# Two hybrid mixer blocks on one core: in the forgetting attention VectorE takes a turned tile's low part ahead of the newest maximum, and GpSimd's norm weights of the gating branch stand at other steps

## The chip, the core and the metric

The kernel runs on one core of a Trainium2 chip. TensorE (PE) multiplies matrices into eight banks of PSUM, VectorE (DVE) and ScalarE (ACT) read those banks, GpSimd (POOL) works in SBUF alone, and SyncE (SP) starts the transfers. Each engine takes its own instructions strictly in the order in which the program lists them; between engines there are only semaphores. The metric is the device time in microseconds (us) of one execution, lower is better.

## The reference, cut to what matters

The whole computes two blocks of width 1024 over 512 tokens, in fp32: a gated delta rule with windowed attention, and then a block with forgetting attention, a chunked spatial gating branch and a convolved feed-forward. The change touches the second block's attention and its gating branch:

```python
def forgetting_attention(q, k, v, log_f):          # 8 heads of 64, 4 query blocks of 128
    c = jnp.cumsum(log_f, axis=1)
    def block(args):
        logits = jnp.einsum('bqhd,bkhd->bhqk', qi, k).astype(jnp.float32) * scale
        logits = logits + ci[..., None] - c_k
        logits = jnp.where(causal, logits, -jnp.inf)
        p = jax.nn.softmax(logits, axis=-1).astype(v.dtype)
        return jnp.einsum('bhqk,bkhd->bqhd', p, v)

def chunked_spatial_gating(u, vg, v_gain, w_s, b_s):
    vg = rmsnorm(vg, v_gain.reshape(G, Dg))        # v_gain: the "norm weights"
    w = w_s * jnp.tril(jnp.ones((CHUNK, CHUNK), dtype=w_s.dtype))
    mixed = jnp.einsum('gij,bnjgd->bnigd', w, vc) + b_s.T[None, None, :, :, None]
    return (u * mixed.reshape(B, S, G, Dg)).reshape(B, S, G * Dg)
```

## The kernel before, in words

Every large product is made exact enough by splitting both factors into a high part (rounded) and a low part (the rest): three matmuls in place of one. ScalarE copies a weight unit's high part (`wh`), GpSimd subtracts it from the raw unit for the low part (`wl`, line 1149), four slots in a ring.

The order of all work is one Python list, ORDER, written out by hand: `do("name", ...)` appends a step, and each engine later runs those steps of the list that it has a function for. So the place of a `do` in the list sets the place of its instructions on every engine at once. A name that only one engine knows moves that engine alone.

The forgetting attention works through 32 tiles n (head n // 4, query block 3 - n % 4, so that the key widths go 512, 384, 256, 128 and again). The loop has 36 steps (lines 942 to 959). For tile n there are these pieces, which the text below calls by letters:

- S(n), TensorE: scores into bank 4 or 5, four matmuls, the last `bank<-nub,idb` (the causal mask). It waits for the exponential of tile n - 2, which reads the same bank.
- M(n), VectorE line 2073: the negated maximum of each row (`mx`).
- E(n), ScalarE: the exponential `p<-bank,mx` with its row sum `dn`. It waits for M(n).
- R(n), VectorE line 2079: the reciprocal of the sum. N(n), GpSimd line 1251: `p<-p,dn`, the normalised tile.
- T(n), TensorE line 2176: p is turned (transposed, `bank<-consts,p`) into bank 6, at step n + 3. It waits for N(n) and, since there is one bank for it, for L(n - 1).
- H(n), ScalarE: the high part of the turned tile (`pth<-bank`). L(n), VectorE: its low part (`ptl<-bank,pth`), which waits for H(n). Both stand at step n + 3, as T(n) does.
- O(h), TensorE: the product with v for head h (`bank<-pth,vv` and `ptl,vv`), at step 4h + 7. It waits for L(4h + 3). ScalarE and VectorE then add its two halves (`att`).

After these, each step holds "sides": one or two quarters of a dense projection (6 matmuls of 512 columns each), and what comes with it: a weight unit's `wh` and `wl`, or the high and low parts of new queries and keys (`qs`, `kh`, `kl`). The gating branch's own steps come from a generator, `gmlp`: squares, sums, then `gm_gain` four times (GpSimd line 1273, `vg<-vg,rparams`), then the root and the norm. On ScalarE a step therefore reads H(n - 3), E(n), and then `wh` or the copies of the sides; on VectorE M(n), L(n - 3), R(n - 1) and then the sides.

Of the kernel before, what the change touches and what calls it, by code (L numbers as in the profile page):

```python
# [197 lines left out]
def program(nc, x, xt, wflat, cfd, ppd, prd, wsd, tbd, seld, out):  # L198
# [176 lines left out]
    def mark(name):  # L375
        marks.append(Mark(nc, name))
        return marks[-1]
# [15 lines left out]
    resid = mark("resid")  # L393
# [36 lines left out]
    do = lambda *a: ORDER.append(a)  # L430
# [19 lines left out]
    def step(g, n=1):  # L450
        for _ in range(n):
            if next(g, "end") == "end":
                return False
        return True

    def in_turn(*gs):
        for g in gs:
            yield from g
# [440 lines left out]
    def qk_units(j):  # L899
        for what in range(2):  # L900
            u = U_QK2[j] + what
            w_ahead(u + 2)
            G.take(("ch", u), (qk_lo, ("k" if what else "q", j)))
            for part in range(4):
                do("ch_part", u, "n1", part)
                if part == 3:
                    do("qk2", j, what)
                    if what:
                        do("twice", j)
                yield  # L910
# [12 lines left out]
    for n, _ in enumerate(in_turn(qk_units(0), qk_units(1))):  # L923
        if n == 3:
            G.take("cum_a", (fg_a, "lt"))
            do("cum_a")
        if n == 7:
            G.take("cum_b", (fg_v, "c"))
            do("cum_b")
        if n == 11:  # L930
            G.over((0, 1, 2, 3))
        if n == 13:
            for b in FA_S + (FA_T, FA_O):
                BANK[("fa", b)] = (b, emptied[b])
            assert BANK[("ch", U_QK2[1] + 1)][0] not in FA_S + (FA_T, FA_O)
            do("fa_s", 0)
    pace = {n: 2 for n in range(7)}
    pace.update({7: 4, 8: 1, 9: 2, 10: 1, 11: 1, 12: 1})
    pace.update({13: 1, 14: 1, 15: 2})
# [2 lines left out]
    for n in range(36):  # L942
        if 0 < n < 32:
            do("fa_s", n)
        if n > 6 and n % 4 == 3:
            do("fa_o", n // 4 - 1)
        if 3 <= n < 35:
            do("fa_t", n - 3)
        if n < 32:
            do("fa_exp", n)  # L950
        if 1 <= n < 33:
            do("fa_norm", n - 1)
        if 8 <= n < 28 and n % 2 == 0 or n > 32:
            step(gg)
        step(sides, pace.get(n, 0))
        if n in (28, 30, 32):
            do("fa_split", n // 2 - 14)
        if n in (29, 31, 33):
            do("fa_low", n // 2 - 14)
# [80 lines left out]
    def pt_at(tile, qb):  # L1040
        return tile[:, 0:qb + 1, qb * 128:(qb + 1) * 128] if qb < 3 else tile[:, 1:5, 0:128]

    def pt_from(n):
        qb = 3 - n % 4
        return psum[turn_bank(n)][:, 0:(qb + 1) * 128].rearrange("p (k n) -> p k n", n=128)
# [609 lines left out]
    def vector_engine(e):  # L1655
        on = On(e)

        def tt(out_, a, b, op, up):
            return e.tensor_tensor(out_, a, b, op).then_inc(up, 1)  # L1659
# [407 lines left out]
                on.wait_ge(*qk_hi.at(("k", j, 1)))  # L2067
                tt(l[64:128, 1, :], bot, k[64:128, 1, :].bitcast(F32), ALU.subtract, qk_lo.up(("k", j)))

        def fa_s(n):  # L2070
            qb, h = 3 - n % 4, n // 4
            on.wait_ge(*fa_p.at(("s", n)))
            e.tensor_reduce(MX2[:, qb, h:h + 1], psum[FA_S[n % 2]][:, 0:(qb + 1) * 128], AX.X, ALU.max, negate=True).then_inc(
                fa_v.up(("mx", n)), 1)
# [3 lines left out]
            on.wait_ge(*fa_a.at(("p", n)))  # L2078
            e.reciprocal(d, d).then_inc(fa_v.up(("r", n)), 1)  # L2079

        def fa_t(n):
            qb = 3 - n % 4
            on.wait_ge(*fa_a.at(("pt", n)))
            if n % 4 == 0 and n:
                on.wait_ge(*fa_p.at(("o", n // 4 - 1)))
            tt(pt_at(PTL, qb), pt_from(n), pt_at(PTH, qb).bitcast(F32), ALU.subtract, fa_v.up(("pt", n)))
# [51 lines left out]
        def finish(tb):  # L2138
# [12 lines left out]
            for n in range(tb // 3, 2):  # L2151
# [3 lines left out]
        return dict(begin=begin, x_split=x_split, conv_rms=conv_rms, scale=scale, split=split, masks=masks, conv=conv, qexp=qexp, gate_dt=gate_dt, gate_beta=gate_beta, gate2=gate2, rope_tables=rope_tables, rope_sq=rope_sq,  # L2155
                    rope_root=rope_root, rope=rope, rope_keys=rope_keys, rope_k=rope_k, rope_t=rope_t, inv_decay=inv_decay, inv_mb=inv_mb, inv_q=inv_q, inv_m=inv_m,
                    inv_mt=inv_mt, inv_x=inv_x, inv_d=inv_d, inv_x7=inv_x7, inv_t=inv_t, swa_s=swa_s, swa_o=swa_o,
                    scan_ks=scan_ks, scan_s=scan_s, scan_oq=scan_oq, scan_out=scan_out, dn_mul=dn_mul, tok=tok, resid=resid_, fa_const=fa_const, forget=forget, cum_b=cum_b, qk2=qk2, fa_s=fa_s,
                    fa_norm=fa_norm, fa_t=fa_t, fa_o=fa_o_, fa_last=fa_last, gm_sum=gm_sum, gm_rec=gm_rec, gm_norm=gm_norm, gm=gm, up_post=up_post, a_prep=a_prep,
                    finish=finish)  # L2160

    def tensor_engine(e):
# [427 lines left out]
        def down_last(tb):  # L2592
# [4 lines left out]
            for n in range(2):  # L2597
                for k in range(18 if tb else 21, 22):
# [6 lines left out]
                    scan_s=scan_s, scan_av=scan_av, cum_a=cum_a, cum_b=cum_b, fa_s=fa_s, fa_t=fa_t, fa_o=fa_o_, gm=gm, down=down, down_last=down_last)  # L2605

    engines = (tensor_engine, scalar_engine, vector_engine, pool_engine, sync_engine)

    def run(engine, e):
# [10 lines left out]
    with nc.Block() as block:  # L2620
        @block.sync
        def _(e):
            run(sync_engine, e)

        @block.scalar
        def _(e):
            run(scalar_engine, e)

        @block.vector
        def _(e):  # L2630
            run(vector_engine, e)

        @block.gpsimd
        def _(e):
            run(pool_engine, e)

        @block.tensor
        def _(e):
            run(tensor_engine, e)
# [37 lines left out]
```

## Time and profile before

| what | us |
|---|---|
| median of 3 runs (923.84 to 924.92) | 923.9 |
| the profiled execution itself | 923.39 |
| its span, first to last instruction | 921.6 |
| TensorE busy | 906.2 (98% of the span) |
| VectorE busy | 481.8 (52%) |
| ScalarE busy | 457.4 (50%) |
| GpSimd busy | 464.1 (50%) |

The profiled execution lasts 1.8 us longer than its span, and lies 0.5 us under the median of the three runs. The attention loop with its tail lies between 393 and 502 us of the span. A matmul that waits shows the idle time before it in brackets; the start times of two matmuls in a row show the whole delay, since the idle time counts only from the modelled end of the one before.

### The profile page before, as it was taken

The numbers are of one execution on the slowest core, as the hardware profiler recorded it, in microseconds if no ns is written. First come the engines' busy times: TensorE is split into PE (matmuls) and PEld (weight loads), VectorE is DVE, ScalarE is ACT, GpSimd is POOL, SyncE is SP. The second block draws the span as 40 slices with busy tenths as digits, with TensorE's granted clock in tenths as the row PEclk, the third lists the DMA queues.
The fourth block names the chain that finished last, engine by engine and source line by source line (L and its number), as shares of the span: only waits on it lengthen the run. The fifth ranks groups of instructions, "written<-read, shape, count | busy, mean of one in ns | idle before, by whom it ended". The sixth has DMA issues, their size and how long they took to land.

```text
span 921.6 us, 11979 instructions
## 1 busy us (share of the span) xinstructions
PE 906.2 (98%) x4752; PEld 763.7 (83%) x4752; DVE 481.8 (52%) x814; ACT 457.4 (50%) x817; POOL 464.1 (50%) x262
## 2 busy tenths in 40 slices
PE   9999999999999999999999999999999999999997
PEld 6988868899999888788777889888888888888885
DVE  4679836898857443533654434333333334654434
ACT  6666587576546444447557245333343433433223
POOL 4453432987566433456786426444444444344440
PEclk9999999999999999999999999999999999999999
DMA  9522310000022714332221214233222233232202
GB/s 344 191 91 91 97 42 1 1 1 2 2 92 68 267 46 137 115 92 70 75 86 46 97 60 132 101 104 101 92 92 92 91 96 110 73 133 93 91 23 92
DMA packets 25303, 83.63 MB, mean 91 GB/s; under 512 B 3008, under 2 KB 3264, under 8 KB 25120
## 3 DMA queue, kind: packets, MB, share of 16 engines
q1 hardware_dynamic: 24240, 81.49, 26.4%
q10 hardware_dynamic: 1008, 1.38, 0.4%
q8 instruction: 38, 0.62, 0.3%
q14 instruction: 17, 0.14, 0.0%
HBM read 78.66 MB, written 2.10 MB: 88 GB/s over the span
## 4 chain that ended last, share of the span: by engine, by line
PE 81%; DVE 9%; POOL 5%; ACT 3%; DMA 1%; issue 1%; SPq 0%; DVEq 0%; ACTq 0%
PE bank L2168 78%; PE bank L2176 3%; DVE qk L1665 2%; DVE vc L1665 1%; POOL mb L1161 1%; POOL wl L1149 1%; DVE r L1659 1%; ACT L1290 1%; DMA xt<-in_xt 1%; POOL mb L1165 1%; POOL p L1251 1%; POOL dd L1171 1%; DVE bank L1659 0%; ACT vc L1290 0%; ACT xh L1290 0%
## 5 line engine op out<-in xcount | busy, mean ns | idle before, releaser
L1149 POOL TENSOR_TENSOR wl<-raw,wh 128x1024 fp32r<-128x1024 f32 (+1 forms) x129 | 310.3, 2410 | 364.0 <-ACT wh L1290 364.0
L2168 PE MATMUL bank<-xh,wh 128*128 128x512 f32 (+1 forms) x536 | 206.8, 386 | 0.0
L2168 PE MATMUL bank<-xl,wh 128*128 128x512 f32 (+1 forms) x536 | 205.2, 383 | 0.0
L2168 PE MATMUL bank<-xh,wl 128*128 128x512 f32 (+1 forms) x528 | 202.2, 383 | 0.0
L1290 ACT ACTIVATE wh<-raw 128x1024 fp32r<-128x1024 f32 (+2 forms) x132 | 136.0, 1035 | 123.9 <-PE bank L2168 117.8
L2168 PE MATMUL bank<-wh,xh 128*128 128x512 f32 (+1 forms) x352 | 140.5, 399 | 0.8 <-POOL wl L1149 0.4
L2168 PE MATMUL bank<-wh,xl 128*128 128x512 f32 (+1 forms) x352 | 134.5, 382 | 0.0
L2168 PE MATMUL bank<-wl,xh 128*128 128x512 f32 (+1 forms) x352 | 134.1, 381 | 0.0
L2168 PEld LDWEIGHTS bank<-xh,wh 128*128 128x128 f32 x536 | 100.8, 188 | 19.3 <-issue 0.2
L2168 PEld LDWEIGHTS bank<-xl,wh 128*128 128x128 f32 x536 | 100.8, 188 | 19.2
L2168 PEld LDWEIGHTS bank<-xh,wl 128*128 128x128 f32 x528 | 99.2, 188 | 19.6
L2168 PEld LDWEIGHTS bank<-wh,xh 128*128 128x128 f32 x352 | 66.3, 188 | 15.5 <-POOL wl L1154 1.7
L1659 DVE TENSOR_TENSOR al<-ac,ah 128x512 fp32r<-128x512 f32 x22 | 53.6, 2450 | 45.8 <-ACT ah L1290 45.8
L2168 PEld LDWEIGHTS bank<-wh,xl 128*128 128x128 f32 x352 | 66.1, 188 | 13.0
L2168 PEld LDWEIGHTS bank<-wl,xh 128*128 128x128 f32 x352 | 66.4, 189 | 11.8 <-issue 1.0
L1665 DVE SCALAR_TENSOR_TENSOR ta<-bank,pparams,ta 128x510 f32<-128x510 f32 (+1 forms) x44 | 32.9, 749 | 74.1 <-ACT ta L1290 73.3
L2168 PE MATMUL bank<-wh,ah 128*128 128x512 f32 x176 | 68.5, 389 | 0.0
L2168 PE MATMUL bank<-wl,ah 128*128 128x512 f32 x176 | 68.5, 389 | 0.0
L2168 PE MATMUL bank<-wh,al 128*128 128x512 f32 x176 | 68.5, 389 | 0.0
L1665 DVE SCALAR_TENSOR_TENSOR tgg<-bank,pparams,tgg 128x510 f32<-128x510 f32 (+1 forms) x44 | 33.0, 749 | 62.4 <-ACT tgg L1290 61.6
L1290 ACT ACTIVATE tgg<-bank,pparams 128x512 f32<-128x512 f32 x22 | 17.2, 781 | 78.8 <-PE bank L2168 78.8
L1251 POOL TENSOR_SCALAR p<-p,dn 128x512 f32<-128x512 f32 (+3 forms) x32 | 34.8, 1089 | 16.8 <-DVE dn L2079 16.7
(271 smaller groups left out, 1424.7 us busy)
## 6 DMA issues: line engine op xcount, KB each, us to landing
raw<-in_wflat SPq DMA_DIRECT2D x126, 512.0 KB, 3.5
xt<-in_xt SPq DMA_DIRECT2D x8, 256.0 KB, 4.4
h<-in_x SPq DMA_DIRECT2D x4, 512.0 KB, 8.1
h<-in_x SPq DMA_DIRECT2D x1, 2048.0 KB, 8.3
gain<-in_pr SPq DMA_DIRECT2D x3, 512.0 KB, 5.0
consts<-in_cf SPq DMA_DIRECT2D x1, 1088.0 KB, 10.5
raw<-in_wflat SPq DMA_DIRECT2D x4, 272.0 KB, 11.0
kh<-kh SPq DMA_DIRECT2D x8, 128.0 KB, 2.3
```

What stands on the lines that cost most here:

```text
L1149: e.tensor_tensor(WL[u % NS][:, 0:n], RAW[u % NS][:, 0:n], WH[u % NS][:, 0:n].bitcast(F32), ALU.subtract).then_inc(w_lo.up(u), 1)
L1161: e.tensor_tensor(h3(mb), h3(mb), bc4((cf("SL"), cf("SU"))[d]), ALU.mult).then_inc(inv_g.up(("mb1", cb, d)), 1)
L1165: e.tensor_tensor(both, both, mb, ALU.add).then_inc(inv_g.up(("mb", cb)), 1)
L1171: e.tensor_tensor(h3(W["DD"][:, lower(d)]), h3(raw(cb)), bc4(cf("LM", d)), ALU.mult).then_inc(inv_g.up(("dd", cb, 0, d)), 1)
L1251: e.tensor_scalar(p, p, DN2[:, qb, h:h + 1], None, ALU.mult).then_inc(fa_g.up(n), 1)
L1290: return e.activation(out_, in_, f, **k).then_inc(up, 1)
L1659: return e.tensor_tensor(out_, a, b, op).then_inc(up, 1)
L1665: return e.scalar_tensor_tensor(out_, a, s, b, op0, op1).then_inc(up, 1)
L2168: return e.matmul(o, l, r_, start=start, stop=stop, skip_group_check=part)
L2176: return e.transpose(o, in_, cf("ident")[0:in_.shape[0], 0:in_.shape[0]])
```

## The change

On VectorE the step `fa_s` is now called `fa_mx` (the maximum) and `fa_t` is called `fa_tl` (the low part), so that they can be placed apart from TensorE's and ScalarE's steps of the old names. In the steps n with n % 4 other than 3 the low part L(n - 3) now stands ahead of M(n); where n % 4 is 3 it stays behind M(n). TensorE's, ScalarE's and SyncE's orders are as before. On GpSimd the four `gm_gain` move from steps 20, 22, 24 and 26 to 21, 23, 25 and 27.

```diff
             do("fa_s", 0)
+            do("fa_mx", 0)
...
     for n in range(36):
         if 0 < n < 32:
             do("fa_s", n)
+        if 3 <= n < 35 and n % 4 != 3:
+            do("fa_tl", n - 3)
+        if 0 < n < 32:
+            do("fa_mx", n)
         if n > 6 and n % 4 == 3:
             do("fa_o", n // 4 - 1)
         if 3 <= n < 35:
             do("fa_t", n - 3)
+        if 3 <= n < 35 and n % 4 == 3:
+            do("fa_tl", n - 3)
         if n < 32:
             do("fa_exp", n)
         if 1 <= n < 33:
             do("fa_norm", n - 1)
-        if 8 <= n < 28 and n % 2 == 0 or n > 32:
+        if 8 <= n < 20 and n % 2 == 0 or 20 < n < 29 and n % 4 == 1 or n in (23, 27) or n > 32:
             step(gg)
...
-        def fa_s(n):
+        def fa_mx(n):
...
-        def fa_t(n):
+        def fa_tl(n):
```

VectorE, steps 12 to 14 of the loop, before: `mx2` is a maximum M, `ptl` a low part L (from bank 6), `dn2` a reciprocal R, `kl0` the low part of new keys.

```order
L1659 TENSOR_TENSOR ptl_242<-bank6,pth_241 128x4x128
L2079 RECIPROCAL dn2_140<-dn2_140 128x1
L2073 TENSOR_REDUCE mx2_139<-bank4 128x1
L1659 TENSOR_TENSOR ptl_242<-bank6,pth_241 128x3x128
L2079 RECIPROCAL dn2_140<-dn2_140 128x1
L2100 TENSOR_REDUCE vss_138<-vsq0_239 128x8
L1659 TENSOR_TENSOR kl0_230<-bank2,kh0_228 64x512 x2
L2073 TENSOR_REDUCE mx2_139<-bank5 128x1
L1659 TENSOR_TENSOR ptl_242<-bank6,pth_241 128x2x128
```

And the same place now, from the same first row:

```order
L1666 TENSOR_TENSOR ptl_242<-bank6,pth_241 128x4x128
L2086 RECIPROCAL dn2_140<-dn2_140 128x1
L1666 TENSOR_TENSOR ptl_242<-bank6,pth_241 128x3x128
L2080 TENSOR_REDUCE mx2_139<-bank4 128x1
L2086 RECIPROCAL dn2_140<-dn2_140 128x1
L2107 TENSOR_REDUCE vss_138<-vsq0_239 128x8
L1666 TENSOR_TENSOR kl0_230<-bank2,kh0_228 64x512 x2
L1666 TENSOR_TENSOR ptl_242<-bank6,pth_241 128x2x128
L2080 TENSOR_REDUCE mx2_139<-bank5 128x1
```

L(9) (3 x 128 wide) has moved ahead of M(12), and L(10) (2 x 128) ahead of M(13); the reciprocal behind each pair keeps its place.

GpSimd, steps 19 to 24, before: `p20` to `p23` are the norms N, `wl3` a weight unit's low part, `vg` a norm weight.

```order
L1251 TENSOR_SCALAR p23_246<-p23_246,dn2_140 128x128
L1273 TENSOR_TENSOR vg_234<-vg_234,rparams_63 128x512
L1149 TENSOR_TENSOR wl3_60<-raw3_52,wh3_56 128x1024
L1251 TENSOR_SCALAR p20_243<-p20_243,dn2_140 128x512
L1251 TENSOR_SCALAR p21_244<-p21_244,dn2_140 128x384
```

And now:

```order
L1251 TENSOR_SCALAR p23_246<-p23_246,dn2_140 128x128
L1149 TENSOR_TENSOR wl3_60<-raw3_52,wh3_56 128x1024
L1251 TENSOR_SCALAR p20_243<-p20_243,dn2_140 128x512
L1273 TENSOR_TENSOR vg_234<-vg_234,rparams_63 128x512
L1251 TENSOR_SCALAR p21_244<-p21_244,dn2_140 128x384
```

The norm weight has gone behind the weight unit's low part and N(20).

## Rows read from the trace of the kernel before

**Rows 1.** The page, part 1: busy us, share of the span, instructions.

```profile
PE 906.2 (98%) x4752; PEld 763.7 (83%) x4752; DVE 481.8 (52%) x814; ACT 457.4 (50%) x817; POOL 464.1 (50%) x262
```

**Rows 2.** TensorE's waits, 390 to 510 us: total us, times, longest.

```profile
PE bank L2176 <- DVE ptl L1659: 1.5, 4, 0.5
```

**Rows 3.** Timeline, steps 15 to 17: start us, us, engine, line, operation, [idle before].

```profile
452.63 1.41 DVE L1665 SCALAR_TENSOR_TENSOR qs<-bank,qs 64x512 fp32r<-64x512 f32 x2 [1.80 <-ACT qs L1290]
...
454.07 0.69 DVE L2073 TENSOR_REDUCE mx<-bank 128x1 f32<-128x512 f32 x1
...
454.80 0.56 DVE L1659 TENSOR_TENSOR ptl<-bank,pth 128x384 fp32r<-128x384 f32 x1
454.80 0.69 ACT L1290 ACTIVATE p<-bank,mx 128x512 f32<-128x512 f32 x1 [1.07 <-DVE mx L2073]
454.81 0.22 PE L2168 MATMUL bank<-nub,idb 128*128 128x128 bf16 x1
...
455.41 0.44 PE L2176 MATMUL bank<-consts,p 128*128 128x128 f32 x2 [0.38 <-DVE ptl L1659]
455.48 1.05 ACT L1290 ACTIVATE wh<-raw 128x1024 fp32r<-128x1024 f32 x1
...
456.83 0.42 DVE L1659 TENSOR_TENSOR ptl<-bank,pth 128x256 fp32r<-128x256 f32 x1 [0.36 <-ACT pth L1290]
...
457.50 0.28 PE L2176 MATMUL bank<-consts,p 128*128 128x128 f32 x1
```

**Rows 4.** Timeline, steps 28 to 30.

```profile
484.89 0.49 PE L2176 MATMUL bank<-consts,p 128*128 128x128 f32 x3
...
485.95 0.56 DVE L1659 TENSOR_TENSOR ptl<-bank,pth 128x384 fp32r<-128x384 f32 x1 [0.16 <-ACT pth L1290]
...
487.44 0.62 ACT L1290 ACTIVATE xh<-att 128x512 fp32r<-128x512 f32 x1
...
488.37 0.42 DVE L1659 TENSOR_TENSOR ptl<-bank,pth 128x256 fp32r<-128x256 f32 x1 [0.42 <-ACT pth L1290]
...
489.17 0.22 PE L2168 MATMUL bank<-nub,idb 128*128 128x128 bf16 x1
489.23 0.28 PE L2176 MATMUL bank<-consts,p 128*128 128x128 f32 x1
```

**Rows 5.** Timeline, steps 12 to 15.

```profile
440.41 0.52 PE L2176 MATMUL bank<-consts,p 128*128 128x128 f32 x3 [0.15 <-POOL p L1251]
...
442.35 1.21 ACT L1290 ACTIVATE kh<-bank 64x512 fp32r<-64x512 f32 x2 [0.22 <-PE bank L2168]
...
442.97 1.41 DVE L1659 TENSOR_TENSOR kl<-bank,kh 64x512 fp32r<-64x512 f32 x2 [0.27 <-ACT kh L1290]
...
445.00 0.42 DVE L1659 TENSOR_TENSOR ptl<-bank,pth 128x256 fp32r<-128x256 f32 x1
445.00 0.58 ACT L1290 ACTIVATE p<-bank,mx 128x384 f32<-128x384 f32 x1 [1.04 <-DVE mx L2073]
...
445.48 0.33 PE L2176 MATMUL bank<-consts,p 128*128 128x128 f32 x1 [0.54 <-DVE ptl L1659]
...
446.82 0.29 DVE L1659 TENSOR_TENSOR ptl<-bank,pth 128x128 fp32r<-128x128 f32 x1 [1.01 <-ACT pth L1290]
...
447.31 0.48 PE L2168 MATMUL bank<-pth,vv 128*128 128x512 f32 x1
```

**Rows 6.** Timeline of ScalarE, steps 6 and 8.

```profile
418.22 0.48 ACT L1290 ACTIVATE p<-bank,mx 128x256 f32<-128x256 f32 x1
...
429.74 1.28 ACT L1290 ACT_TABLE_LOAD   x1
```

**Rows 7.** Timeline of GpSimd: steps 8 and 20.

```profile
428.64 2.39 POOL L1149 TENSOR_TENSOR wl<-raw,wh 128x1024 fp32r<-128x1024 f32 x1 [3.38 <-ACT wh L1290]
...
466.76 1.31 POOL L1273 TENSOR_TENSOR vg<-vg,rparams 128x512 f32<-128x512 f32 x1
```

**Rows 8.** Timeline of TensorE, step 23.

```profile
472.03 0.66 PE L2176 MATMUL bank<-consts,p 128*128 128x128 f32 x4 [0.61 <-POOL p L1251]
```

More of the change, by code:

```diff
@@ L2157, in vector_engine @@
                     inv_mt=inv_mt, inv_x=inv_x, inv_d=inv_d, inv_x7=inv_x7, inv_t=inv_t, swa_s=swa_s, swa_o=swa_o,
-                    scan_ks=scan_ks, scan_s=scan_s, scan_oq=scan_oq, scan_out=scan_out, dn_mul=dn_mul, tok=tok, resid=resid_, fa_const=fa_const, forget=forget, cum_b=cum_b, qk2=qk2, fa_s=fa_s,
-                    fa_norm=fa_norm, fa_t=fa_t, fa_o=fa_o_, fa_last=fa_last, gm_sum=gm_sum, gm_rec=gm_rec, gm_norm=gm_norm, gm=gm, up_post=up_post, a_prep=a_prep,
+                    scan_ks=scan_ks, scan_s=scan_s, scan_oq=scan_oq, scan_out=scan_out, dn_mul=dn_mul, tok=tok, resid=resid_, fa_const=fa_const, forget=forget, cum_b=cum_b, qk2=qk2, fa_mx=fa_mx,
+                    fa_norm=fa_norm, fa_tl=fa_tl, fa_o=fa_o_, fa_last=fa_last, gm_sum=gm_sum, gm_rec=gm_rec, gm_norm=gm_norm, gm=gm, up_post=up_post, a_prep=a_prep,
                     finish=finish)
```

## The prediction

> **What bounds the kernel now.** I read the page first: TensorE is busy for 98% of the span [rows 1], so almost nothing can be won but the moments in which a matmul waits, and whatever makes TensorE wait longer is lost in full. Then TensorE's waits in the stretch of the attention loop, the only one where the change moves anything: four turns T wait for VectorE's low part L, 1.5 us in all [rows 2], and two for GpSimd's norm N, 0.15 and 0.61 us [rows 5, 8]. Last the timelines of all engines around these waits, where the reader is to see two things.
>
> First, why L comes late. In step 16 VectorE takes the new queries' low part, then M(16), then L(13), and T(14) stands still for L(13) [rows 3]. The idle time shown is 0.38 us, but the last matmul ahead of T(14) starts at 454.81 and T(14) at 455.41; with nothing to wait for, T follows that matmul by 0.06 us (489.17 and 489.23 in step 30 [rows 4]). So the real price is 0.54 us. Step 20 repeats the pattern to a hundredth. In step 13 it is T(11) at 445.48 behind L(10) at 445.00, with keys in place of queries, and costs 0.7 us (0.54 idle and the same hidden 0.16) [rows 5].
>
> Second, what M feeds. E(16) starts in the instant in which M(16) ends, having waited 1.07 us for it; `wh` follows E, the copy H(14) follows `wh`, L(14) follows H at 456.83, and it ends at 457.25, only 0.25 us ahead of T(15) [rows 3]. So M(16) begins a chain over ScalarE that leads back to the next turn, and the slack of this chain is 0.2 us.
>
> **The change, part by part.** Nothing is added or removed; 24 low parts and 24 maxima change places in pairs, and four norm weights move by a step each. Per pair L gains the time of M (0.69 us at 512 columns) and M loses the time from its own readiness to L's end. Where H(n - 3) is not ready, which is the usual case, M no longer runs in that shadow: it waits for T, H and L. All sums are start to start.
>
> 1. The waits that go. With L(13) at 454.07, where M(16) was, it ends at 454.63, ahead of T(14)'s free place at 454.87: -0.54 in step 16, -0.53 in step 20 [rows 3].
>
> 2. The same steps, one turn later. M(16) now starts behind L(13), 0.5 us later (0.56 less a small overlap, an estimate), at 454.57. From M to E 0.73, E to `wh` 0.68, `wh` to L(14) 1.35, L(14) to its turn 0.48 [rows 3, 5]: T(15) can start at 457.81. Its free place is 0.54 ahead of the 457.50 of before, at 456.96. So it waits 0.85, and the two steps together are 0.31 us worse than before. Steps 20 and 21 likewise: +0.85.
>
> 3. Steps 24 and 28, where before nothing waited. The loop is now T to L 1.06 [rows 4], L to M 0.5, M to E 0.73, E to `wh` 0.68, `wh` to L 1.35, L to T 0.48: 4.80 us for two turns. TensorE needs 489.23 - 484.89 = 4.34 [rows 4]. Step 24: +0.46. In step 28 a copy `xh` stands between `wh` and H: `wh` to `xh` is 0.95 (its 1.05 less the overlap), `xh` to L(26) 0.93 [rows 4], in place of 1.35, so the loop is 5.33: +0.99.
>
> 4. Step 12 to 15. The loop there runs through keys: T(9) to L(9) 1.06, then M(12) 0.5, E 0.73, the copies `kh` 0.68, `kl` 0.62 behind (442.35 to 442.97), L(10) 1.44 behind that, T(11) 0.48 [rows 3 to 5]. That is 5.51 from T(9). From 440.41 it gives 445.92 where T(11) was at 445.48 [rows 5]: +0.44, although the wait for M is gone. Then E(13), at 445.00 before, is late by 1.9 (0.5 late from the move, the rest from L(10)), and with it `wh`, H(11) and L(11), which stood at 446.82: it ends at 449.0. O(2) needs it, and its free place is 447.31 + 0.97 = 448.28 [rows 5]. So O(2) waits +0.8. (The 0.97 is this 0.44 and the 0.53 of point 5.)
>
> 5. Upstream of that. E(6) at 418.22 followed H(3) at once and now waits for L(3) and M(6) too, 0.2 (0.29 less an overlap) and 0.42 by the lengths of an L of these widths [rows 3, 5], about 0.6, less 0.1 for which ScalarE idles afterwards. From there to the `wh` for which GpSimd waits at 428.64 ScalarE has almost no gap, and from 428.64 to N(9) GpSimd has none; T(9) already waits for N(9) by 0.15 [rows 5 to 7]. So T(9) comes +0.53 later. From both sides: 0, if ScalarE has slack that I don't see, and 0.6.
>
> 6. Norm weights. T(20) waits 0.61 for N(20) [rows 8], since GpSimd puts a norm weight of 1.31 ahead of the weight's low part and N(20) [rows 7]. Behind N(20) it is out of the way. Most of the wait goes, -0.6: not more, as point 2 makes `wh` and so GpSimd's own loads late in the same step. The other three have slack on both sides of a step: 0. If ScalarE's lateness took all of the freed time, this would be 0.
>
> Sum: -0.54 - 0.53 + 0.85 + 0.85 + 0.46 + 0.99 + 0.44 + 0.8 + 0.53 - 0.6 = +3.25 us. The profiled execution took 923.39, so 926.6 by its own measure; the median of the runs is 0.5 above it, which makes 927.1, and I state 927.0. Behind the loop TensorE runs on without waits of this size, so nothing gives the time back.
>
> One cover deserves a word. In step 8 ScalarE loads its exponential table, 1.28 us from 429.74 [rows 6], while M(8) runs behind L(5); both are ready within 0.1 us of each other, so I cost step 8 at nothing. The Trainium skill (ScalarE: Activation LUTs, "What ACT_TABLE_LOAD costs") gives a switch 2.66 us, the load and a drain. The row shows the load alone; by the page M(8) would be covered with over a microsecond to spare, and the sum would be the same but its rival below, a load that waits for M, dearer: 2.66 in place of 1.28.
>
> **The rivals.** *The waits simply go (faster).* L is what T waits for, so L first is right, and ScalarE absorbs the later E. Then TensorE wins 0.54 + 0.53 + 0.59 (step 13: from `kl`'s end at 444.38 VectorE ran M(13) until L(10) at 445.00 [rows 5]) + 0.6 for N(20), 2.3 us: 921.6 by the median. For it: three of the four waits are of this kind [rows 2], and VectorE and ScalarE are half idle over the span [rows 1]. Against it: it needs E(16) late by 0.5 to leave L(14) in time, and L(14) has 0.25 [rows 3]. It decides from there: a lateness of E under 0.2 us costs nothing, above it all goes to the next turn.
>
> *Losses and gains cancel (no change).* Points 4 and 5 lie upstream of each other; if the `kh` copies of step 12 get ahead, or ScalarE has slack, what is left is -1.07 + 1.70 + 1.45 - 0.6 - 0.59 = +0.9 us: 924.8. For it: 1.8 us of my sum hang on two delays that feed each other. Against it: ScalarE takes its work in order, and in step 12 E(12) stands ahead of `kh` in a place where `kh` had waited only 0.22 for TensorE [rows 5].
>
> *The lateness compounds (slower still).* N is late as well in steps 19, 23 and 28, since `wh` carries GpSimd's `wl` with it: 0.2 each, and the table load in step 8 waits for M(8), 1.28 more [rows 6]. That gives 3.25 + 0.6 + 1.28 = 5.1: 929.0. Against it: nothing in the order ties the load to M.
>
> **How the numbers follow.** Forecast 0.62, faster 0.12, cancelling 0.17, compounding 0.09. A measurement of this kernel tells about 0.2%, 1.8 us, from no change. The forecast's own range is 925.5 to 928.4: 1.5 off if T(9) does not slip (0.5), O(2) slips by half (0.4) and the two loops of point 3 are 0.3 shorter each, 1.4 on if the norms slip too (0.6) and ScalarE frees nothing in point 6 (0.6) and hands on another 0.2. To leave out no more than 2 in 10 the range reaches down through part of the cancelling case and up into the compounding one: 923.5 to 928.8. Slower by over 0.2% (above 925.7) takes the compounding case and nearly all of the forecast, 0.70; within 0.2% takes the cancelling case and a little of the forecast, 0.17; faster 0.13.
>
> **What would show it.** In the profile after: M(16), M(20), M(24), M(28) start behind L and not ahead of it; E waits for M in every step but the fourth; T(14) and T(18) show no wait, but T(15), T(19), T(23) and T(27) wait for L by 0.4 to 1.0 us; O(2) waits for L(11); TensorE's waits for L grow from 1.5 us in 4 to some 4 us in 8 or so, and those for N shrink only if point 6 outweighs point 5. The forecast is wrong if T(15) starts without a wait, or if T(9) stays where it was and T(11) comes earlier.

## The result, and the profile after

The changed kernel takes 927.08 us (median of 7 runs, 926.48 to 928.77) against 924.04 us (7 runs) for the kernel before, run beside it. The ratio is 1.0031, with a 95% interval of 1.002 to 1.0042: 1.8 to 3.9 us slower. The prediction said 927.0 and slower with a chance of 0.70. The profiled execution took 926.48 us, 3.1 more than that of before.

From the page of the changed kernel, the line that answers to [rows 1]:

```profile
PE 906.0 (98%) x4752; PEld 763.6 (83%) x4752; DVE 480.0 (52%) x814; ACT 457.8 (50%) x817; POOL 464.4 (50%) x262
```

TensorE does the same work; it stands still for longer. Its waits between 390 and 514 us (total us, times, longest), against the 1.5 us for L of [rows 2]:

```profile
PE bank L2183 <- DVE ptl L1666: 3.6, 6, 1.0
PE bank L2175 <- DVE ptl L1666: 0.8, 2, 0.6
PE bank L2183 <- POOL p L1258: 0.3, 1, 0.3
```

Four waits for a low part have become eight (L2183 is a turn T, L2175 a product O), and the two for a norm [rows 5, 8] have become one, that of T(9). T(20) no longer waits.

All kernels of this study do the same work in the same order up to T(0), and yet T(0) stands at 406.53 us before, at 406.33 after, and as late as 410.13 in another kernel's trace. So I measure each turn from T(0) of its own trace. In the loop two traces of different kernels then agree to 0.01 us up to T(7), and to 0.06 us up to T(26) where nothing ahead of it was changed. The table gives how much later than before (a minus: earlier) some turns and products start, counted so; 0 stands for 0.03 and less. Its first column is the running sum that the prediction's terms give, the others are the changed kernel and the kernels of the experiments below.

| | predicted | after | low parts alone | weights alone | three steps | wh one later | low, wh two later | wh two later | best |
|---|---|---|---|---|---|---|---|---|---|
| O(1) | 0 | +0.39 | +0.39 | 0 | 0 | +0.38 | +0.38 | 0 | 0 |
| T(9) | +0.53 | +0.52 | +0.54 | 0 | 0 | +0.52 | +0.52 | 0 | 0 |
| T(11) | +0.97 | +0.93 | +0.95 | 0 | -0.62 | +0.92 | +0.93 | 0 | -0.61 |
| O(2) | +1.77 | +1.71 | +1.73 | 0 | +0.16 | +0.93 | +0.92 | 0 | -0.61 |
| T(14) | +1.23 | +1.19 | +1.25 | 0 | -0.34 | +0.40 | +0.41 | 0 | -1.14 |
| T(15) | +2.08 | +2.01 | +2.06 | 0 | +0.47 | +0.35 | +0.35 | 0 | -1.20 |
| O(3) | +2.08 | +2.06 | +2.11 | 0 | +0.52 | +1.10 | +0.35 | 0 | -1.20 |
| T(18) | +1.55 | +1.63 | +1.70 | 0 | +0.12 | +0.55 | -0.23 | -0.06 | -1.78 |
| T(19) | +2.40 | +2.45 | +2.51 | 0 | +0.93 | +0.50 | -0.28 | -0.07 | -1.84 |
| T(20) | +1.80 | +1.86 | +2.06 | -0.74 | +0.49 | +0.50 | -1.05 | -0.83 | -2.61 |
| T(23) | +2.26 | +2.28 | +2.48 | -0.72 | +0.49 | +1.05 | -1.08 | -0.88 | -2.63 |
| T(27) | +3.25 | +3.23 | +3.58 | -0.92 | +0.49 | +1.76 | -1.28 | -1.08 | -2.83 |
| O(7) | +3.25 | +3.28 | +3.65 | -0.91 | +0.50 | +4.29 | -0.20 | -1.07 | -2.82 |

After O(7) nothing moves: from there to the end of the span it is 422.1 us in both traces (921.6 - 499.50 and 924.7 - 502.58). In the other traces the span from T(0) to the end, too, is longer or shorter by what the last row says, within 0.11 us.

The prediction, and one expectation below, speak of 24 maxima and low parts that change places. It is 21 pairs: in steps 32 to 34 there is a low part and no maximum. No term of the sum uses the number.

The timeline of steps 15 to 17 after, to be laid beside [rows 3]:

```profile
454.16 1.41 DVE L1672 SCALAR_TENSOR_TENSOR qs<-bank,qs 64x512 fp32r<-64x512 f32 x2 [1.80 <-ACT qs L1297]
...
455.61 0.56 DVE L1666 TENSOR_TENSOR ptl<-bank,pth 128x384 fp32r<-128x384 f32 x1
...
456.08 0.68 DVE L2080 TENSOR_REDUCE mx<-bank 128x1 f32<-128x512 f32 x1
...
456.40 0.39 PE L2183 MATMUL bank<-consts,p 128*128 128x128 f32 x2
...
456.80 0.69 ACT L1297 ACTIVATE p<-bank,mx 128x512 f32<-128x512 f32 x1 [1.53 <-DVE mx L2080]
...
457.47 1.05 ACT L1297 ACTIVATE wh<-raw 128x1024 fp32r<-128x1024 f32 x1
...
458.42 0.37 ACT L1297 ACTIVATE pth<-bank 128x256 fp32r<-128x256 f32 x1
...
458.83 0.42 DVE L1666 TENSOR_TENSOR ptl<-bank,pth 128x256 fp32r<-128x256 f32 x1 [1.41 <-ACT pth L1297]
...
459.31 0.33 PE L2183 MATMUL bank<-consts,p 128*128 128x128 f32 x1 [0.71 <-DVE ptl L1666]
```

The row to see is T(14), 456.40: it has lost its wait in brackets, as the change wants. Follow the others down: L(13), M(16) at its heels, E(16) which idled 1.53 us for it (1.07 before), `wh`, H(14), L(14), and T(15) now waits 0.71 for that. From the first `qs` row to T(15) it is 5.15 us; before it was 4.87, wait of T(14) included.

### The profile page after: what moved, and what is told of

It reads as the page before. It is cut to its first block, busy times and chain, and to the rows that moved or that the text cites. A ratio compares the mean times of both kernels' runs of the same rounds, so it can differ in the third digit from the quotient of the medians.

```text
span 924.7 us, 11979 instructions
## 1 busy us (share of the span) xinstructions
PE 906.0 (98%) x4752; PEld 763.6 (83%) x4752; DVE 480.0 (52%) x814; ACT 457.8 (50%) x817; POOL 464.4 (50%) x262
## 4 chain that ended last, share of the span: by engine, by line
PE 79%; DVE 10%; ACT 5%; POOL 4%; issue 1%; DMA 1%; SPq 0%; DVEq 0%; ACTq 0%
PE bank L2175 76%; PE bank L2183 3%; DVE qk L1672 2%; DVE vc L1672 1%; POOL mb L1168 1%; ACT L1297 1%; ACT wh L1297 1%; DVE r L1666 1%; POOL wl L1156 1%; DVE ptl L1666 1%; POOL mb L1172 1%; DMA xt<-in_xt 1%; POOL dd L1178 1%; ACT p L1297 1%; DVE bank L1666 0%
## 5 line engine op out<-in xcount | busy, mean ns | idle before, releaser
L2175 PE MATMUL bank<-xh,wh 128*128 128x512 f32 (+1 forms) x536 | 206.8, 386 | 0.0
L2175 PE MATMUL bank<-xl,wh 128*128 128x512 f32 (+1 forms) x536 | 205.2, 383 | 0.0
L2175 PE MATMUL bank<-xh,wl 128*128 128x512 f32 (+1 forms) x528 | 202.2, 383 | 0.0
L2175 PE MATMUL bank<-wh,xh 128*128 128x512 f32 (+1 forms) x352 | 140.3, 399 | 1.6 <-DVE xl L1672 1.3
L2175 PE MATMUL bank<-wh,xl 128*128 128x512 f32 (+1 forms) x352 | 134.5, 382 | 0.0
L2175 PE MATMUL bank<-wl,xh 128*128 128x512 f32 (+1 forms) x352 | 134.1, 381 | 0.0
L2175 PEld LDWEIGHTS bank<-xh,wh 128*128 128x128 f32 x536 | 100.9, 188 | 19.5 <-issue 0.2
L2175 PEld LDWEIGHTS bank<-xl,wh 128*128 128x128 f32 x536 | 100.8, 188 | 19.2
L2175 PEld LDWEIGHTS bank<-xh,wl 128*128 128x128 f32 x528 | 99.3, 188 | 19.4
L2175 PEld LDWEIGHTS bank<-wh,xh 128*128 128x128 f32 x352 | 66.4, 189 | 15.7 <-POOL wl L1161 2.1
L2175 PEld LDWEIGHTS bank<-wh,xl 128*128 128x128 f32 x352 | 66.1, 188 | 13.1
L2175 PEld LDWEIGHTS bank<-wl,xh 128*128 128x128 f32 x352 | 66.3, 188 | 11.6 <-issue 1.0
L2175 PE MATMUL bank<-wh,ah 128*128 128x512 f32 x176 | 68.5, 389 | 0.0
L2175 PE MATMUL bank<-wl,ah 128*128 128x512 f32 x176 | 68.5, 389 | 0.0
L2175 PE MATMUL bank<-wh,al 128*128 128x512 f32 x176 | 68.5, 389 | 0.0
```

The costliest lines, as they stand in the source:

```text
L2175: return e.matmul(o, l, r_, start=start, stop=stop, skip_group_check=part)
```

## The experiments

Each diff is against the changed kernel, and each table value is counted from T(0), as above.

### Low parts alone

```diff
-        if 8 <= n < 20 and n % 2 == 0 or 20 < n < 29 and n % 4 == 1 or n in (23, 27) or n > 32:
+        if 8 <= n < 28 and n % 2 == 0 or n > 32:
```

> Low parts ahead of the maxima as in the changed kernel, the four norm weights left where they were. Chain theory (a late maximum delays the exponential, the weight's high part, the next high part H, the next low part L, the next turn T): slower than before by 3.3 + 0.4 = 3.7 us; T(20) comes 2.2 us later than before (1.9 in the changed kernel), as the norm weight again stands ahead of the weight's low part and N(20), but ScalarE's lateness had already used up most of that room. Rival (GpSimd and the moved norm weights make the loss): no slower than before, since the waits for L at T(11), T(14), T(18) go: -1.7 us.

Measured: ratio 1.0047 (1.0035 to 1.0059), +4.3 us; by the table +3.65, of which T(20) +2.06. The loss is that of the low parts. Counted from the turn before, the norm weights' move saves 0.14 us at T(20) and 0.15 at T(24) (the two columns are 0.06 apart already at T(19), from T(13) on, where no norm weight has moved), not the 0.6 that I had put down for it. The row of the changed kernel in step 20, and then three of this one:

```profile
469.71 2.37 POOL L1156 TENSOR_TENSOR wl<-raw,wh 128x1024 fp32r<-128x1024 f32 x1 [1.07 <-ACT wh L1297]
```

```profile
469.89 0.61 POOL L1258 TENSOR_SCALAR p<-p,dn 128x128 f32<-128x128 f32 x1 [2.27 <-DVE dn L2086]
470.46 1.28 POOL L1280 TENSOR_TENSOR vg<-vg,rparams 128x512 f32<-128x512 f32 x1
471.71 2.37 POOL L1156 TENSOR_TENSOR wl<-raw,wh 128x1024 fp32r<-128x1024 f32 x1
```

In the changed kernel GpSimd idles 1.07 us for the late `wh`. Here it runs the norm weight (1.25 us, start to start) in that time. So nearly all of the wait at T(20) was gone by T(19)'s own lateness.

### Norm weights alone

```diff
-        if 3 <= n < 35 and n % 4 != 3:
+        if 3 <= n < 35 and False:
...
-        if 3 <= n < 35 and n % 4 == 3:
+        if 3 <= n < 35 and not (False):
```

> Norm weights moved alone, maxima ahead of low parts as before. Chain theory: the wait of 0.61 us (0.72 start to start) at T(20) goes and 0.2 at T(24): 0.7 to 0.9 us faster than before, at the edge of what can be measured. Rival (the norm weights carry the loss): slower by 1 to 3 us.

Measured: ratio 0.9996 (0.9987 to 1.0004), -0.4 us and not to be told from nothing; in the trace T(20) is 0.74 and T(24) 0.89 us earlier, and all behind them. As expected, and no rival to the low parts. T(20) without its wait, against [rows 8]:

```profile
471.22 0.66 PE L2183 MATMUL bank<-consts,p 128*128 128x128 f32 x4
```

### The swap only where a turn had waited

```diff
-        if 3 <= n < 35 and n % 4 != 3:
+        if 3 <= n < 35 and n in (13, 16, 20):
```

with the other condition its negation, and norm weights as before.

> The low part goes ahead of the maximum only in steps 13, 16 and 20, the three where TensorE waited for a low part behind a maximum; norm weights as before. Chain theory: each wait goes and comes back larger one turn or product later: O(2) +0.2, T(15) +0.3, T(19) +0.3, so 0.8 us slower than before, with T(11), T(14), T(18) without a wait and O(2), T(15), T(19) with one. Rival (the swap is good where a turn waited and bad only where it was made for nothing, as in steps 6, 9, 12, 24 and 28): 0.59 + 0.54 + 0.53 = 1.7 us faster than before.

Measured: ratio 1.001 (1.0001 to 1.0019), +0.9 us; by the table +0.50. The rival falls: three waits taken away, and the kernel is no faster. Two of the waits that came in their place (O(2) and T(15)):

```profile
447.65 0.50 PE L2175 MATMUL bank<-pth,vv 128*128 128x512 f32 x1 [0.58 <-DVE ptl L1666]
...
458.15 0.33 PE L2183 MATMUL bank<-consts,p 128*128 128x128 f32 x1 [0.71 <-DVE ptl L1666]
```

T(11) is 0.62 earlier and O(2) 0.16 later; T(14) gains 0.54 on T(13) (+0.20), and T(15) loses 0.81. I had said +0.8. At T(19) it is +0.93, of which 0.18 lie between T(15) and T(16) (+0.65), which starts as N(16) ends; this I had left out. T(20) gives 0.44 back, as it would have waited for N(20) anyhow.

### The weight's high part one quarter later, then two

The chain theory says that the 0.95 us of `wh` between E and H are what closes the loop. So the changed kernel was run with the weight units' steps (load, `wh`, `wl`) from step 13 on listed one quarter of a projection later:

```diff
-            w_ahead(u + 2)
+            if u < 51:
+                w_ahead(u + 2)
             G.take(("ch", u), (qk_lo, ("k" if what else "q", j)))
             for part in range(4):
+                if part == 1 and u >= 51:
+                    w_ahead(u + 2)
...
-            w_ahead(u0 + i + 2)
+            if u0 != U_U2:
+                w_ahead(u0 + i + 2)
             for tb in range(4):
+                if tb == 1 and u0 == U_U2:
+                    w_ahead(u0 + i + 2)
```

> The changed kernel with one edit: from step 13 on the weight unit's load, high and low part (ScalarE, GpSimd) are listed one quarter of a projection later, so that ScalarE makes H and the next exponential ahead of the weight's high part. Chain theory: the 0.95 us of the high part leave the chain from maximum to next turn; the loop of steps 24 and 28 is 3.9 us against TensorE's 4.3, so T(15), T(19), T(23), T(27) and O(2) stop waiting, and N(20), N(24) stand ahead of the weight's low part. Left is +0.97 up to T(11) less 0.54, 0.53, 0.72 and 0.18: 1.0 us faster than before, 4 us faster than the changed kernel. Rival (the swap itself costs, through late maxima and norms, whatever ScalarE does next): still 2 to 3 us slower than before.

Measured: ratio 1.0052 (1.004 to 1.0064), +4.8 us; by the table +4.29. This expectation failed. The turns that I had named do stop waiting (T(15) +0.35 in place of +2.01, and T(19), T(23), T(27) by the table). But `wh` now stands one place further down ScalarE's queue, between E(17) and H(15), and the head's product needs L(15):

```profile
458.73 0.58 ACT L1303 ACTIVATE p<-bank,mx 128x384 f32<-128x384 f32 x1 [0.96 <-DVE mx L2086]
...
459.30 1.04 ACT L1303 ACTIVATE wh<-raw 128x1024 fp32r<-128x1024 f32 x1
...
460.25 0.26 ACT L1303 ACTIVATE pth<-bank 128x128 fp32r<-128x128 f32 x1
...
460.54 0.29 DVE L1672 TENSOR_TENSOR ptl<-bank,pth 128x128 fp32r<-128x128 f32 x1 [1.78 <-ACT pth L1303]
...
460.89 0.50 PE L2181 MATMUL bank<-pth,vv 128*128 128x512 f32 x1 [0.56 <-DVE ptl L1672]
```

That is the same chain, one member on: M(17), E(17), `wh`, H(15), L(15), O(3). And GpSimd's `wl` went between N(20) and N(21), N(24) and N(25), N(28) and N(29), where the next turn does need the second of them:

```profile
476.19 0.52 PE L2189 MATMUL bank<-consts,p 128*128 128x128 f32 x3 [0.40 <-POOL p L1264]
...
498.63 0.52 PE L2189 MATMUL bank<-consts,p 128*128 128x128 f32 x3 [1.20 <-POOL p L1264]
```

A product's low part `xl` stands ahead of N(29) as well.

So the same again with two quarters (step 13's still one), to steps 18, 22, 26 and 30, where ScalarE idles ahead of the head's product:

```diff
+                if part == 1 and u == 51 or part == 2 and u == 52:
+                    w_ahead(u + 2)
...
+            late = u0 == U_U2 and i < 3
+            if not late:
+                w_ahead(u0 + i + 2)
             for tb in range(4):
+                if late and tb == 2:
+                    w_ahead(u0 + i + 2)
```

> All 24 swaps of the changed kernel and its norm weights, but the weight unit's part of step 13 one quarter later and those of steps 16, 20, 24 and 28 two quarters later, so that neither H(n - 3) of the next step nor the last H of a head stands behind it. Chain theory: T(15), T(19), T(23), T(27), O(2) and O(3) to O(6) don't wait; left is the +0.93 of T(11), less 0.54, 0.53, 0.7 and 0.2: about 1.0 us faster than before, at T(27) and before it. The norms of steps 30 and 31 may be late by up to 1 us (T(29)). Rival (late maxima cost wherever the high part of the weight stands): 2 us or more slower than before.

Measured: ratio 1.0006 (0.9996 to 1.0015), so level with before, and 2.5 per mille under the changed kernel's 1.0031. In the table T(27) is 1.28 us earlier than before, 4.5 earlier than in the changed kernel, with all the swaps in place. The last turns give 1.1 of it back. T(29) waits for L(28) by 0.88: ScalarE runs without a gap from E(30), late at 492.22, over `wh` (492.68), a copy `xh` and an `att` to H(28) at 494.90. And `wl` of step 30 stands ahead of N(30). Both are read from the trace, and no run tests them. I had expected a loss here, but from the norms alone. Its waits in the loop:

```profile
PE bank L2190 <- DVE ptl L1673: 1.8, 2, 0.9
PE bank L2190 <- POOL p L1265: 0.3, 1, 0.3
PE bank L2182 <- DVE ptl L1673: 0.2, 1, 0.2
```

The swap therefore does not cost by itself. It costs by what ScalarE does between the late exponential and the next H: where that is still the key copies, T(11), the +0.93 stays.

The two quarters alone (steps 16, 20, 24 two, step 13 one, step 28 as it was; orders of VectorE and norm weights as before):

> Orders of VectorE and norm weights as before; only the weight unit's part of step 13 goes one quarter later and those of steps 16, 20 and 24 two. Chain theory: the waits for L at T(11), T(14), T(18) stay as they are, those for N at T(20) and T(24) go: 0.9 us faster than before. Rival (the place of the weight's high part is itself the gain, whatever the maxima do): 2 us faster or more.

Measured: ratio 0.9996 (0.9987 to 1.0005); by the table -1.07, nearly all of it at T(20) and T(24). So with `wh` two quarters later the swaps cost nothing up to T(27) (-1.28 with them, -1.08 without, though norm weights and step 28's `wh` differ too). The waits for L stay as in [rows 2]:

```profile
PE bank L2190 <- DVE ptl L1673: 1.5, 4, 0.5
```

### Single swaps

Each is the kernel before with one swap: the changed kernel's `n % 4 != 3` replaced by one step, and the norm weights back where they were. Each is a single run, read by its trace. The whole times, 926.46 (step 28), 926.43 (step 12) and 925.89 us (step 6) against 925.29 for one run of the kernel before, decide nothing.

> The kernel before with one swap, L(25) ahead of M(28) in step 28, where nothing waited. By the loop T(25), H, L, M(28), E(28), weight's high part, copy xh, H(26), L(26), T(27) of 5.33 us against TensorE's 4.34: T(27) is 1.0 us later after T(0) than before, and all ahead of it as before. Rival (the swap costs only where lateness has piled up from earlier swaps): T(27) as before.

> The kernel before with one swap, L(9) ahead of M(12) in step 12. By the chain T(9), H, L, M(12), E(12), the key copies on ScalarE, the key's low part on VectorE, L(10): T(11) 0.4 us later than before, T(9) as before, and O(2) up to 0.3 later again, since E(13), the weight's high part and L(11) follow. Rival (T(11)'s lateness comes from GpSimd's backlog at T(9)): T(11) as before.

> The kernel before with one swap, L(3) ahead of M(6) in step 6. By point 5 of the prediction E(6) comes 0.6 us later, ScalarE hands that on to the weight's high part at 427.5 us and GpSimd, without a gap, to N(9): O(1) as before, T(9) 0.5 us later, and all behind it 0.5 us later. Rival (the lateness of T(9) came with O(1), from the swap in step 9): T(9) as before.

T(27) of the first, T(11) of the second, T(9) of the third:

```profile
492.23 0.33 PE L2183 MATMUL bank<-consts,p 128*128 128x128 f32 x1 [0.77 <-DVE ptl L1666]
```

```profile
448.48 0.33 PE L2183 MATMUL bank<-consts,p 128*128 128x128 f32 x1 [1.54 <-DVE ptl L1666]
```

```profile
442.87 0.52 PE L2183 MATMUL bank<-consts,p 128*128 128x128 f32 x3 [0.68 <-POOL p L1258]
```

Step 28: T(27) +0.97 and T(26) still +0.04, so 0.93 from one to the other, and the loop holds with no lateness piled up before it. Step 12: T(11) +0.99, where I expected +0.4, and O(2) no later than that, where I had allowed 0.3 more. I had forgotten that with step 13 unswapped M(13), 0.59 start to start, still stands between the late keys and L(10); 0.4 and 0.59 are the 0.99. Step 6: T(9) +0.52 and O(1) unmoved, so the lateness of T(9) does come from E(6) through ScalarE and GpSimd's backlog.

The changed kernel without the swaps of steps 4 to 10:

> The changed kernel without the swaps of steps 4 to 10. By my account the lateness of T(9) comes from the swap in step 6 over ScalarE and GpSimd's backlog: O(1) and T(9) are as before (+0.0 in place of +0.39 and +0.52), and T(11) then depends on its own chain over the key copies alone: +0.44 against before in place of +0.93, T(15) and all after it 0.5 us earlier than in the changed kernel. Rival (T(11) is late by the same chain whatever T(9) does): T(11) still +0.9.

Measured in one run's trace (the run took 929.75 us, 2.7 more than the changed kernel's median, but its T(0) stands 3.8 us later than the changed kernel's): O(1) and T(9) as before, T(11) +0.38, O(2) +1.16, T(27) +2.72 (the changed kernel: +0.93, +1.71, +3.23). The two parts of the early loss add, 0.52 and 0.4.

### Put together

The swap in steps 13, 16 and 20 only; the weight unit's steps two quarters later in steps 16, 20 and 24 and one in step 13, as in the kernel of the two quarters alone; norm weights at steps 19, 23, 24 and 27, where GpSimd would wait for a reciprocal. Against the changed kernel:

```diff
-        if 3 <= n < 35 and n % 4 != 3:
+        if 3 <= n < 35 and n in (13, 16, 20):
...
-        if 8 <= n < 20 and n % 2 == 0 or 20 < n < 29 and n % 4 == 1 or n in (23, 27) or n > 32:
+        if 8 <= n < 20 and n % 2 == 0 or n in (19, 23, 24, 27) or n > 32:
```

> Put together from what the runs showed: low part ahead of the maximum in steps 13, 16 and 20 alone; the weight unit's load, high and low part of step 13 go one quarter of a projection later, those of steps 16, 20 and 24 two quarters (to steps 18, 22 and 26, where ScalarE has idle time ahead of the head's product O); norm weights at steps 19, 23, 24 and 27. Chain theory: the waits of T(11), T(14), T(18), T(20), T(24) go and nothing takes their place: -0.6, -0.5, -0.5, -0.7, -0.2, together 2.5 us faster than before (the waits of T(9) and T(29) stay). Rival (each lateness turns up at some other turn, as it did one quarter later): between -1 and +3 us, with new waits of O for L or of T for N.

Measured: 922.5 us (12 runs) against 923.95 (29 runs), ratio 0.9974 (0.9964 to 0.9984), 1.5 to 3.3 us faster than the kernel before; by the table -2.82. The interval rests on all runs; the two medians alone lie 1.5 us apart, the two means 2.2. It beats both kernels. Of TensorE's waits in the loop one is left in the view:

```profile
PE bank L2190 <- DVE ptl L1673: 0.2, 1, 0.2
```

And its steps 16 to 18:

```profile
456.38 0.39 PE L2190 MATMUL bank<-consts,p 128*128 128x128 f32 x2
...
456.77 0.69 ACT L1304 ACTIVATE p<-bank,mx 128x512 f32<-128x512 f32 x1 [1.53 <-DVE mx L2087]
...
457.45 0.37 ACT L1304 ACTIVATE pth<-bank 128x256 fp32r<-128x256 f32 x1
...
457.85 0.42 DVE L1673 TENSOR_TENSOR ptl<-bank,pth 128x256 fp32r<-128x256 f32 x1
...
458.41 0.28 PE L2190 MATMUL bank<-consts,p 128*128 128x128 f32 x1
...
459.53 1.04 ACT L1304 ACTIVATE wh<-raw 128x1024 fp32r<-128x1024 f32 x1
```

E(16) idles the same 1.53 us for its maximum as in the changed kernel. H(14) now follows it at once, `wh` runs in time that ScalarE had free, and neither T(14) nor T(15) waits. The swap in step 16 loses 0.27 us with `wh` in the chain (three steps: T(13) +0.20, T(15) +0.47) and wins 0.6 (T(13) -0.60, T(15) -1.20) without it.

## Why the prediction was right, point by point

1. *The waits that go.* Right: -0.54 and -0.53 forecast, -0.54 and -0.55 measured (T(13) +1.73 to T(14) +1.19, T(17) +2.18 to T(18) +1.63).
2. *The same steps, one turn later.* Right: +0.85 each forecast, +0.82 measured. The rows show each member, and the run with the swap in three steps shows it apart from all else.
3. *Steps 24 and 28.* Right: +0.46 and +0.99 forecast, +0.41 and +0.94 measured, +0.93 with the swap in step 28 alone (T(26) +0.04, T(27) +0.97).
4. *Steps 12 to 15.* T(11) +0.44 forecast, +0.41 measured; O(2) +0.8 forecast, +0.78 measured. What I left out is that L(7) is late for O(1), too, from the swap in step 9 (+0.39; E(9) idles 0.96 us for M(9), and no run has this swap alone). It costs nothing here, since T(9) has to wait for N(9) anyway.
5. *Upstream.* Right in place and size: +0.53 forecast, +0.52 measured, and step 6 alone gives it.
6. *Norm weights.* T(20) -0.6 forecast and -0.59 measured (T(19) +2.45, T(20) +1.86), but with a wrong account: low parts alone without the move had 0.45 of it. So the move is worth 0.3 us in the changed kernel, at T(20) and T(24), and 0.9 in the kernel before. That the term came out in size is luck.

That the stated 927.0 meets the median of 927.08 to a tenth is luck as well: the seven runs lie between 926.48 and 928.77. What the account carries is the sum, +3.25 forecast and +3.28 at O(7).

The cover in step 8 held. M(8) ran behind the start of the table load, so the load doesn't wait for the maximum, and this part of the compounding rival had no ground:

```profile
429.02 0.49 ACT L1297 ACTIVATE pth<-bank 128x384 fp32r<-128x384 f32 x1
429.53 1.28 ACT L1297 ACT_TABLE_LOAD   x1
430.83 0.69 ACT L1297 ACTIVATE p<-bank,mx 128x512 f32<-128x512 f32 x1
```

```profile
430.02 0.68 DVE L2080 TENSOR_REDUCE mx<-bank 128x1 f32<-128x512 f32 x1
```

The load starts 0.02 us after the copy ahead of it ends, and the exponential follows the load by 1.30 us, start to start, while the Trainium skill (ScalarE: Activation LUTs, "What ACT_TABLE_LOAD costs") gives 2.66 us for a switch with its drain. Here the measurement decides.

The rival of the waits that simply go was the tempting one, and its condition was the right question: it asked whether a later exponential leaves the next low part in time, and L(14) had a quarter of a microsecond for half a microsecond of lateness. The cancelling rival would have needed slack on ScalarE between 418 and 429 us, and the rows had shown none. Of what I said would show it, one figure was too narrow: T(15), T(19), T(23) and T(27) got their waits, but with 0.26 to 0.78 us idle, T(23)'s under the 0.4 that I gave (start to start it loses 0.41). T(14) and T(18) lost theirs, and the total for L came to 4.4 us in 8 waits, as said.

## What to carry to other kernels

A wait names what came last, not what should move: before an instruction is put ahead of another on its engine, follow the one that is put back, over every engine that takes its work in order, to the next thing that the bound engine needs, and compare its delay with the slack there. Here M was given back half a microsecond against a slack of a quarter, and each wait came back larger one turn later. When such a chain closes, the member to move is the long one with the latest deadline (here a weight's preparation, not needed before the next unit is done), and it goes to where its engine idles, not one place down, where it becomes a member of the same chain for the next tile.

## What the runs showed that I had not expected

In a kernel whose bound engine never idles for long, two traces agree to 0.01 us over 28 us (T(0) to T(7)) and to 0.06 over 80 us, once they are counted from a common event, although T(0) itself lies anywhere from 406.33 to 410.13 us. Terms of 0.2 us could be read from single profiles, where 11 timed runs of the kernel with the norm weights alone, against 23 of the kernel before, left an interval 1.6 us wide (0.9987 to 1.0004). And lateness on a full engine was hardly damped and not amplified: 0.6 us at E(6) was 0.5 at T(9) more than 20 us later, through a dozen instructions of ScalarE and eight of GpSimd.
